# Head gates of an mLSTM layer projected ahead of the heads as 2x2 block products, on one Trainium2 core

## The chip, the core and the metric

One core of a Trainium2 chip runs the whole kernel. The metric is device time in microseconds (us). The kernel before was run three times; its median is the time before. Every profile is one profiled execution. About 0.2% (4.1 us) is what a measurement of this kernel can tell from no change.

## What is computed

Two layers of a hybrid backbone over T = 1152 tokens (128 context, 1024 latent) of width D = 1024. Layer 0 mixes by RG-LRU and Fourier groups, layer 1 by an mLSTM of 8 heads (key width 128, value width 256) that runs in chunks of 128 tokens in both directions. The change is in layer 1:

```python
def mixer_c(h, C0, n0, m0, w_in, b_if, w_out):
    proj = h @ w_in
    q, k, v, o, z, gp = jnp.split(proj, [QK_C, 2*QK_C, 2*QK_C+W_C, 2*QK_C+2*W_C, 2*QK_C+3*W_C], axis=-1)
    ...
    for d in range(2):                     # two directions
        hd, Cd, nd, md = mlstm_chunkwise(fl(q), fl(k), fl(v), fl(gp[:, :, d, 0]), fl(gp[:, :, d, 1]), ...)
        hsum = hsum + fl(hd)
    y = jax.nn.sigmoid(o) * hsum.astype(h.dtype) * jax.nn.silu(z)
    return y @ w_out, ...
```

Per head, o and z are each 256 columns wide: two tiles of 128 columns each. "Pair u" below is o tile u and z tile u, u = 0 to 15, two pairs to a head.

## The kernel before

Activations lie transposed, channels on partitions and the 1152 tokens in the free dimension, for KC = 8 blocks of channels. Every fp32 product is made of three products of fp32r parts: hi by hi, hi by lo, lo by hi. The parts of layer 1's input, `h2hi` and `h2lo` (tiles `h_hi`, `h_lo` in the trace), are made once in the stage `outputs(0, ...)`.

`project` (L116 to L128) makes one output tile of 128 channels by 1152 tokens: 8 blocks times 3 parts times 3 banks of 384 columns, 72 matmuls (L126), into one of two PSUM groups. Its weight tile goes through a ring of two slots: `w_load` (L95, SP) brings 128x1024 into `w_raw`, `w_split_hi` (L102, ACT, the copy in L107) makes `w_hi` when it is loaded and when PE has done with the tile two before (`w_used`), `w_split_lo` (L109, DVE, L111) makes `w_lo`, and `project` waits for `w_lo`. Tiles have sequence numbers: the gate projection (input and forget gates of all heads) is 32, and mLSTM's jobs begin at SEQ0 = 33.

`mlstm()` (L1536 on) runs `body(j, ...)` nine times: body 0 projects head 0 and computes the decays of all heads; body j projects head j and, between its products, does the recurrent work of head j-1; body 8 does the last head's recurrence and its gates. A body's jobs on PE are 0 for q, 1 for k, 2 and 3 for v (`values`, L1867, 256-column matmuls, 72 to a job, both jobs read both v weight tiles) and 4 to 7 for z, o, z, o, by `project`. Nine `step`s (L1832 to L1850: state product and numerators of one chunk in each direction; DVE: L2127 to L2148) stand between the jobs or in a job's middle, so that DVE updates the state while PE projects. ACT (`on_scalar`, L1944 to L2004) takes each product out of PSUM, then splits the tile two further on. The gates: tanh and copy from PSUM by ACT (L1972 to L1975), `gate_z` and `gate_o` on DVE (L2156, L2160) into `out_gate`, which `finish_y` (L2118) multiplies with the turned output. All orders are written out by hand; nothing is scheduled by a program.

Decays: `forget_gates` (L2013 to L2058, with log1p in L551 to L563) is a chain of small operations on `[40, 1152]` rows on DVE, with the splits of v's weight tiles hooked in by name ("inverted", "series_ready", "added"). Its input is the gate projection, copied by ACT to `gate_products` (L2003) and moved to rows by four DMAs (L1674). `gates_to_tokens` (L1786, PE) and `token_scalars` (L2064, DVE) hand the result to the heads.

```python
                    steps(4, 5)
                    split(7)
                    gate(j, 0)
                    steps(6, 7)
                    split(8)
```

These lines of DVE's body before show how weight splits (`split(n)` is `w_split_lo` of job n, n > 7 the next body's) stand between the steps.

Of the kernel before, what the change touches and what calls it, by code (L numbers as in the profile page):

```python
# [14 lines left out]
ds = bass.ds  # L15
# [32 lines left out]
def build(nc, a, out):  # L48
# [253 lines left out]

    def setup():
# [12 lines left out]
        const_in, vec_in, prm_rows_in = sem("const_loaded"), sem("vectors_loaded"), sem("lru_vectors_loaded")  # L316
# [3 lines left out]
        vec_turned, vec_ready = sem("vectors_turned"), sem("vectors_ready")  # L320
        x_turned, xT_dve, xT_act = (sem(s) for s in ("x_turned", "xT_by_dve", "xT_by_act"))
        cond_tanh, cond_ready, zero_ready = sem("cond_tanh"), sem("cond_ready"), sem("zeros_ready")
        x_summed, x_std, x_rstd, x_scaled = (sem(s) for s in (
            "x_rows_squared", "x_rows_std", "x_rows_rstd", "x_rows_scaled"))
        mod_rows, mod_turned, mod_ready, wm_used = (sem(s) for s in (
            "mod_rows_ready", "mod_turned", "mod_ready", "w_mod_used"))
        dve_chain = sem("setup_dve_chain")
# [34 lines left out]
        def on_tensor(pe):  # L362
# [29 lines left out]
            for t in range(NT):  # L392
                pe.wait_ge(x_scaled, t + 1)
# [4 lines left out]
                ins.then_inc(x_turned, 1)  # L398
# [20 lines left out]
        def on_scalar(act):  # L419
# [6 lines left out]
            def x_copy(t):  # L426
                act.wait_ge(x_turned, t + 1)
                act.activation(XT[:, :, t * P:(t + 1) * P].rearrange("p (b k) n -> p b k n", b=2), turned_x(t),
                               ACT.Copy).then_inc(xT_act, 1)
# [24 lines left out]
            for t in range(NT):  # L454
# [5 lines left out]
                act.activation(STD[:, t:t + 1], SSQ[:, t:t + 1], ACT.Sqrt, scale=1.0 / D, bias=EPSB[:]).then_inc(x_std, 1)  # L460
# [23 lines left out]
        def on_vector(dve):  # L484
            ch = Chain(dve, dve_chain)

            def x_copy(t):
                dve.wait_ge(x_turned, t + 1)
# [38 lines left out]
            for t in range(NT):  # L527
                dve.wait_ge(x_std, t + 1)
                dve.reciprocal(STD[:, t:t + 1], STD[:, t:t + 1]).then_inc(x_rstd, 1)
                dve.wait_ge(x_rstd, t + 1)  # L530
                dve.tensor_scalar(XR[:, t, :], XR[:, t, :], STD[:, t:t + 1], None, ALU.mult).then_inc(x_scaled, 1)
# [67 lines left out]
    pads = sem("pads_zero")  # L599
# [600 lines left out]
    def outputs(l, next_tiles):  # L1200
# [32 lines left out]
        def first_products(pe, k0, k1):  # L1233

            if l and k0 == 0:
                pe.wait_ge(mlstm_evacuated, 8 * H)
# [10 lines left out]
        def on_sync(sp):  # L1247
# [54 lines left out]
            if next_tiles:  # L1302
                w_load(sp, *at_seq(SEQ + 2), next_tiles[2])
                w_load(sp, *at_seq(SEQ + 3), next_tiles[3])
# [222 lines left out]

    DK, DV = P, 2 * P
    DV1 = DV + 1
    QCOL, KCOL, VCOL, OCOL, ZCOL = 0, D, 2 * D, 4 * D, 6 * D  # L1530
    SEQ0 = 33
# [9 lines left out]
    def mlstm():  # L1541
# [4 lines left out]
        G = sb("out_gate", [P, 2 * T], at=z)  # L1546
        TO = sb("o_tanh", [P, T], at=z)
        TZ = sb("z_tanh", [P, T], at=z)
        GP_ROWS = sb("gate_products", [P, T], at=list(z))
# [29 lines left out]
        small_in, rows_sb = sem("gate_small_loaded"), sem("gates_in_sbuf")  # L1579
# [26 lines left out]
        def pair(j, n):  # L1606

            if isinstance(j, int):
                return at_seq(SEQ0 + n if j == 0 else SEQ0 + 8 * j - 4 + n - (4 if j == H else 0))
            return j * 4 + (SEQ0 - 4 + n) // 2, (SEQ0 - 4 + n) % 2  # L1610

        def jobs(j):
            return range(4) if isinstance(j, int) and j == 0 else range(4, 8) if isinstance(j, int) and j == H else range(8)

        FIRST_JOBS = {(0, 1): 1, (0, 2): 0, (0, 3): 1, (1, 0): 0, (1, 1): 1}
# [4 lines left out]
        def group_free(eng, j, n):  # L1620
            if isinstance(j, int) and (j, n) == (0, 1):
# [723 lines left out]
```

## Time and profile before

| what | value |
|---|---|
| median of 3 runs | 2047.18 us (2046.47 to 2047.83) |
| span of the profiled execution | 2045.1 us |
| its own time less its span | about 2.1 us, as far as the median tells |
| PE busy | 2010.5 us, 98% of the span |
| DVE, ACT, POOL busy | 1062.9, 652.1 and 106.1 us |

PE is the engine with hardly any idle time. A line of the profile names engine, source line and tiles; "PE MATMUL psum_groups<-h_hi,w_hi" is a product of tokens with weights, the last operand being the stationary one.

### The profile page before, as it was taken

How to read it: one execution, taken by the hardware profiler on the slowest of the kernel's cores; microseconds unless marked ns; L12 is line 12 of the kernel's file. 1: busy time of each engine (PE TensorE's matmuls, PEld its weight loads, DVE VectorE, ACT ScalarE, POOL GpSimd, SP SyncE). 2: the span in 40 equal slices, each digit the busy share in tenths (PEclk: the TensorE clock that was granted, in tenths of full speed). 3: DMA queues.
4: the chain of work that ended last, by engine and by line, in shares of the span. 5: the costliest groups of instructions: out<-in, count | busy, mean ns of one | idle time of the engine just before them, and what ended most of it. 6: DMA issues, size and time to landing. Idle time of an engine off the chain costs nothing.

```text
span 2045.1 us, 28555 instructions
## 1 busy us (share of the span) xinstructions
PE 2010.5 (98%) x11833; PEld 1886.1 (92%) x11833; DVE 1062.9 (52%) x1664; ACT 652.1 (32%) x831; POOL 106.1 (5%) x99
## 2 busy tenths in 40 slices
PE   6999999999999999999999999999999999999998
PEld 5999999999988888999999999999999999998887
DVE  5778788445453575853434335343343433645344
ACT  6677764222234453221111111111121111224422
POOL 0032332000200000000000000000000000000000
PEclk9999999999999999999999999999999999999999
DMA  8221213542246443141222212212122121426554
GB/s 302 68 66 46 74 47 94 184 174 83 73 154 186 154 164 118 42 117 30 83 71 81 62 32 84 70 59 78 38 83 61 48 94 42 104 67 189 170 174 140
DMA packets 218346, 204.62 MB, mean 100 GB/s; under 512 B 13346, under 2 KB 187002, under 8 KB 218098
## 3 DMA queue, kind: packets, MB, share of 16 engines
q1 hardware_dynamic: 214194, 190.52, 30.1%
q0 software_dynamic: 3872, 12.35, 1.8%
q8 instruction: 89, 1.46, 0.3%
q14 instruction: 31, 0.25, 0.0%
q10 hardware_dynamic: 160, 0.05, 0.0%
HBM read 172.14 MB, written 30.59 MB: 99 GB/s over the span
## 4 chain that ended last, share of the span: by engine, by line
PE 93%; ACT 2%; DVE 2%; DMA 1%; issue 1%; SPq 1%; DVEq 0%; ACTq 0%
PE psum_groups L126 48%; PE psum_groups L1229 19%; PE psum_groups L1867 10%; PE psum_groups L1848 3%; PE psum_extra L1839 3%; PE psum_groups L1850 3%; PE psum_groups L1008 1%; PE psum_groups L701 1%; PE psum_groups L144 1%; PE psum_groups L1808 1%; PE psum_groups L998 1%; PE psum_extra L1022 1%; DMA w_mod_rows_a<-in_w_mod 1%; ACT gate_i L762 1%; PE psum_groups L1819 1%
## 5 line engine op out<-in xcount | busy, mean ns | idle before, releaser
L126 PE MATMUL psum_groups<-h_hi,w_hi 128*128 128x384 f32 x1896 | 447.8, 344 | 2.5 <-ACT q_t L1958 1.8
L126 PE MATMUL psum_groups<-h_lo,w_hi 128*128 128x384 f32 x1896 | 434.3, 337 | 0.0
L126 PE MATMUL psum_groups<-h_hi,w_lo 128*128 128x384 f32 x1896 | 434.1, 337 | 0.0
L126 PEld LDWEIGHTS psum_groups<-h_hi,w_hi 128*128 128x128 f32 x1896 | 338.8, 188 | 11.9 <-issue 7.8
L126 PEld LDWEIGHTS psum_groups<-h_lo,w_hi 128*128 128x128 f32 x1896 | 340.5, 188 | 0.0
L126 PEld LDWEIGHTS psum_groups<-h_hi,w_lo 128*128 128x128 f32 x1896 | 340.0, 188 | 0.0
L1229 PE MATMUL psum_groups<-w_out,y_tile_hi 128*128 128x512 f32 x1008 | 317.4, 394 | 0.0
L1229 PEld LDWEIGHTS psum_groups<-w_out,y_tile_hi 128*128 128x128 f32 x1008 | 189.6, 188 | 42.5
L2132 DVE SCALAR_TENSOR_TENSOR state<-state,head_decay,psum_extra 128x257 f32<-128x257 f32 x112 | 54.1, 483 | 287.9 <-PE psum_groups L1850 285.9
L1229 PE MATMUL psum_groups<-w_out,y_tile_lo 128*128 128x512 f32 x504 | 198.1, 393 | 0.0
L1867 PE MATMUL psum_groups<-w_hi,h_hi 128*128 128x256 f32 x576 | 164.4, 285 | 0.0
L1867 PE MATMUL psum_groups<-w_hi,h_lo 128*128 128x256 f32 x576 | 162.5, 282 | 0.0
L1867 PE MATMUL psum_groups<-w_lo,h_hi 128*128 128x256 f32 x576 | 162.3, 282 | 0.0
L111 DVE TENSOR_TENSOR w_lo<-w_raw,w_hi 128x1024 fp32r<-128x1024 f32 x97 | 133.8, 1379 | 47.5 <-ACT w_hi L107 39.1
L107 ACT ACTIVATE w_hi<-w_raw 128x1024 fp32r<-128x1024 f32 x97 | 102.5, 1057 | 46.8 <-PE psum_groups L1867 35.8
L1229 PEld LDWEIGHTS psum_groups<-w_out,y_tile_lo 128*128 128x128 f32 x504 | 94.8, 188 | 20.9
L1867 PEld LDWEIGHTS psum_groups<-w_hi,h_hi 128*128 128x128 f32 x576 | 108.6, 189 | 1.5 <-ACT v_rows L1962 1.5
L1867 PEld LDWEIGHTS psum_groups<-w_lo,h_hi 128*128 128x128 f32 x576 | 108.7, 189 | 0.0
L1867 PEld LDWEIGHTS psum_groups<-w_hi,h_lo 128*128 128x128 f32 x576 | 108.5, 188 | 0.0
L1972 ACT ACTIVATE z_tanh<-psum_groups 128x1152 f32<-128x1152 f32 x16 | 18.1, 1132 | 253.2 <-PE psum_groups L126 253.2
L273 DVE TENSOR_TENSOR y_tile_lo<-y_tile_raw,y_tile_hi 128x512 fp32r<-128x512 f32 x126 | 80.0, 686 | 34.3 <-ACT y_tile_hi L269 33.9
L1848 PE MATMUL psum_groups<-v_rows,decay_matrix 128*128 128x257 f32 x288 | 84.8, 380 | 0.0
(331 smaller groups left out, 2448.0 us busy)
## 6 DMA issues: line engine op xcount, KB each, us to landing
w_raw<-in_w_in_o SPq DMA_DIRECT2D x65, 512.0 KB, 4.9
y_tile_raw<-y_scratch SPq DMA_DIRECT2D x126, 256.0 KB, 3.0
w_raw<-in_w_in_e SPq DMA_DIRECT2D x32, 512.0 KB, 4.0
w_mod_rest<-in_w_mod SPq DMA_DIRECT2D x4, 4096.0 KB, 15.3
y_scratch<-mixed_y POOLq DMA_DIRECT2D x16, 576.0 KB, 3.2
decay_matrix<-gate_rows SPq DMA_DIRECT2D x8, 1152.0 KB, 7.6
q_carry<-gate_rows SPq DMA_DIRECT2D x8, 1152.0 KB, 6.4
y_scratch<-out_gate SPq DMA_DIRECT2D x8, 1152.0 KB, 5.2
```

Of the source, the lines that this page charges most:

```text
L107: act.activation(WHI[:, slot, :], WRAW[:, slot, :], ACT.Copy).then_inc(w_hi, 1)
L111: dve.tensor_tensor(WLO[:, slot, :], WRAW[:, slot, :], WHI[:, slot, :].bitcast(F32), ALU.subtract).then_inc(w_lo, 1)
L126: ins = pe.matmul(PS[:, group, j, 0:JW], w[:, slot, k * P:(k + 1) * P], h(k0 + k)[:, j * JW:(j + 1) * JW], start=start and k == 0 and m == ...
L144: ins = pe.matmul(bank, w[:, slot, k * P:(k + 1) * P], h(k0 + k)[:, g * JW:(g + 1) * JW], start=start and k == 0 and m == 0, stop=stop and ...
L273: eng.tensor_tensor(y_lo_at(l, n, c), y_raw_at(l, n, c), y_hi_at(l, n, c).bitcast(F32), ALU.subtract).then_inc(yo_lo, 1)
L701: ins = pe.matmul(PS[:, what, j, 0:JP + 1], w[:, 2 * what + d, :], x[:, j * JP:(j + 1) * JP + 1], start=m == 0, stop=m == 2)
L1229: ins = pe.matmul(bank(n), y, w[part], start=k == 0 and m == 0, stop=k == 2 * KC - 1 and m == 2)
L1839: ins = pe.matmul(KV[d][:, 0:DV1], KW[:, d, t * P:(t + 1) * P], V[q][:, t, :], start=True, stop=True)
L1848: ins = pe.matmul(NUM[d][:, 0:DV1], DM[q][:, d, cols], V[q][:, t, :], start=True, stop=s == 0)
L1850: ins = pe.matmul(NUM[d][:, 0:DV1], QW[:, d, cols], C[:, d, :], start=False, stop=True)
L1867: ins = pe.matmul(dst, h[:, k, t * P:(t + 1) * P], w[:, slot, cols], start=k == 0 and m == 0 and n % 2 == 0, stop=k == KC - 1 and m == 2, ...
L2132: ins = dve.scalar_tensor_tensor(C[:, d, :], C[:, d, :], DC[:, d, tiles[d]:tiles[d] + 1], KV[d][:, 0:DV1], ALU.mult, ALU.add)
```

## The change

It adds a stage `o_z_gates()` between layer 0's outputs and `mlstm()`. There the gates of heads 0 to 6 (pairs 0 to 13) are computed and stored in DRAM (`gate_scratch`); mLSTM loads two pairs per head. Pair 0 is made by two plain products. Pairs 1 to 13 are each a 2x2 block product, (o and z columns) by (two halves of the channels) by (two halves of the tokens), by the Strassen-Winograd scheme: 7 products of 512 channels by 128 columns by 576 tokens (24 matmuls of 288 columns each) where two plain ones took 8 quarter products of that size. Four sums of token quarters are made once (128x2304 each, hi and lo), four sums of weights for every pair, and five sums of the products. Head 7's gates stay where they were. Bodies 0 to 7 have 4 jobs instead of 8 (q, k, v, v), and the nine steps are set inside these jobs. The gate projection goes through DRAM on its way to rows. DVE and SP begin mLSTM after the stage's last product.

```diff
-    def project(pe, pair, slot, group, hi, lo, k0=0, start=True, stop=True, ready=None, middle=None, ks=range(KC)):
+    def project(pe, pair, slot, group, hi, lo, k0=0, start=True, stop=True, ready=None, middle=None, ks=range(KC), at=None):
...
+            if at and k in at:
+                at[k]()
...
+        MOVING = [(tokens(H2HI, 0, FIRST_Q), tokens(H2LO, 0, FIRST_Q)), (THI[T2], TLO[T2]), (THI[T1], TLO[T1]),
+                  (tokens(H2HI, 1, FIRST_Q), tokens(H2LO, 1, FIRST_Q)), (THI[T3], TLO[T3]),
+                  (tokens(H2HI, 1, SECOND_Q), tokens(H2LO, 1, SECOND_Q)), (THI[T4], TLO[T4])]
...
+        def on_gpsimd(pool):
+            outputs_over(pool)
+            pool.tensor_tensor(TRAW[T1][:], tokens(H2LO, 0, SECOND_Q).bitcast(F32), tokens(H2LO, 0, FIRST_Q).bitcast(F32),
+                               ALU.subtract).then_inc(t_pool[0], 1)
+            pool.wait_ge(*since(t_lo, 1))
+            pool.tensor_tensor(TRAW[T4][:], tokens(H2HI, 1, FIRST_Q).bitcast(F32), TRAW[T4][:], ALU.subtract
+                               ).then_inc(t_pool[0], 1)
...
+            project(pe, *at_seq(34), 1, h2hi, h2lo)
+            for u in range(1, GU):
+                for p in range(PRODUCTS):
...
+                    for k in range(4):
+                        for m, (wn, hn) in enumerate(((0, 0), (0, 1), (1, 0))):
+                            for j in range(2):
+                                ins = pe.matmul(BANKS[p][:, j, :], w[wn][:, k * P:(k + 1) * P],
+                                                h[hn][:, k, j * JQ:(j + 1) * JQ], start=OPENS[p] and k == 0 and m == 0,
+                                                stop=k == 3 and m == 2, skip_group_check=True)
+                    ins.then_inc(product_done[0], 1)
...
+        def on_vector(dve):
...
+            for u in range(1, GU):
+                if u > 1:
+                    combined(u - 1, 5)
+                operand(u, 4)
+                if u > 1:
+                    z_part(u - 1)
+                operand(u, 5)
+                combined(u, 1)
...
-    SEQ0 = 33
+    SEQ0 = 35
...
         def on_sync(sp):
-            outputs_over(sp)
+            gates_over(sp)
...
+                elif qkv:
+                    job(0, {4: turn_k})
+                    scores()
+                    job(1, {3: turn_before, 5: do_step(0)})
+                    do_step(1)()
+                    job(2, {2: do_step(2), 4: do_step(3), 6: do_step(4)})
+                    do_step(5)()
+                    job(3, {3: do_step(6), 6: do_step(7)})
+                    do_step(8)()
...
-                    at_hooks = {"inverted": 3, "series_ready": 4, "added": 5}
+                    at_hooks = {"inverted": 2, "series_ready": 3, "scanned": 4}
...
-            outputs_over(dve)
+            gates_over(dve)
...
+            dve.wait_ge(gate_stored, 16 * GU)
             run(dve, body, Heads())
```

Where the instructions go, at three places.

DVE at the start of the new stage, behind layer 0's last pieces. `token_sum_218`, `220`, `221` are raw sums of token quarters (T1, T3 and T4, T4's buffer holding T2 first), `token_sum_lo_215` is the lo part of T2, `weight_sum_222` and `223` sums of quarters of the o and z weights, which lie in `w_raw` here; L1791 makes a lo part of a weight operand.

```order
L1487 TENSOR_TENSOR h_lo<-psum_extra,h_hi 128x8x128 [waits h2_hi_ready]
L111 TENSOR_TENSOR w_lo<-w_raw,w_hi 128x1024 [waits w_hi_ready]
L1825 TENSOR_TENSOR token_sum_220<-h_hi 128x2304 [waits h2_lo_ready,x_stored]
L1825 TENSOR_TENSOR token_sum_220<-token_sum_220,h_lo 128x2304 [waits setup_then_gate_dve_chain] x2
L1825 TENSOR_TENSOR token_sum_221<-token_sum_220,h_hi 128x2304 [waits mod_turned_then_token_sum_ready]
L1825 TENSOR_TENSOR token_sum_221<-token_sum_221,h_lo 128x2304 [waits setup_then_gate_dve_chain]
L1780 TENSOR_TENSOR weight_sum_222<-w_raw 128x512 [waits vectors_loaded_then_o_z_weights_loaded_1]
...
L1791 TENSOR_TENSOR strassen_weights_lo<-w_raw,strassen_weights_hi 128x512 [waits x_rows_rstd_then_strassen_weights_hi,x_rows_scaled_then_weight_sum_ready]
...
L1795 TENSOR_TENSOR token_sum_lo_215<-token_sum_221,token_sum_hi_211 128x2304 [waits cond_tanh_then_token_sum_hi]
L1791 TENSOR_TENSOR w_lo<-weight_sum_223,w_hi 128x512 [waits x_rows_rstd_then_strassen_weights_hi]
L1825 TENSOR_TENSOR token_sum_218<-token_sum_218,h_hi 128x2304 [waits vectors_ready_then_token_sum_by_pool]
...
L1791 TENSOR_TENSOR w_lo<-weight_sum_222,w_hi 128x512 [waits x_rows_rstd_then_strassen_weights_hi]
```

None of these rows exists before, where memsets of mLSTM's rows follow layer 0's last row (there L1478) and the `L111`. Each lo of a token sum stands behind ACT's hi of the same sum, and the two raw operations on T1 (`token_sum_218`, one shown) behind the first lo.

DVE in a head's last steps, before. A pair of `state` rows opens a step, a pair of `h_rows` rows ends it; the split is that of job 7, and the gates of a pair follow it.

```order
L2132 SCALAR_TENSOR_TENSOR state<-state,head_decay,psum_extra 128x257 [waits mlstm_dve_chain]
...
L2145 SCALAR_TENSOR_TENSOR h_rows<-psum_groups,inverse_den,h_rows 128x256 [waits mlstm_dve_chain]
...
L2145 SCALAR_TENSOR_TENSOR h_rows<-psum_groups,inverse_den,h_rows 128x256 [waits mlstm_dve_chain]
...
L111 TENSOR_TENSOR w_lo<-w_raw,w_hi 128x1024 [waits w_hi_ready]
...
L2156 SCALAR_TENSOR_TENSOR out_gate<-z_tanh,out_gate 128x1152 [waits projection_evacuated]
...
L2160 SCALAR_TENSOR_TENSOR out_gate<-o_tanh,out_gate 128x1152 [waits mlstm_dve_chain]
...
L2132 SCALAR_TENSOR_TENSOR state<-state,head_decay,psum_extra 128x257 [waits numerator_done]
...
L2132 SCALAR_TENSOR_TENSOR state<-state,head_decay,psum_extra 128x257 [waits mlstm_dve_chain]
```

The same engine at the same steps in the changed kernel: steps 5 and 6 of a head of the loop.

```order
L2503 SCALAR_TENSOR_TENSOR state<-state,head_decay,psum_extra 128x257 [waits numerator_done]
...
L2516 SCALAR_TENSOR_TENSOR h_rows<-psum_groups,inverse_den,h_rows 128x256 [waits mlstm_dve_chain]
...
L2516 SCALAR_TENSOR_TENSOR h_rows<-psum_groups,inverse_den,h_rows 128x256 [waits mlstm_dve_chain]
...
L111 TENSOR_TENSOR w_lo<-w_raw,w_hi 128x1024 [waits w_hi_ready]
...
L2503 SCALAR_TENSOR_TENSOR state<-state,head_decay,psum_extra 128x257 [waits numerator_done]
...
L2503 SCALAR_TENSOR_TENSOR state<-state,head_decay,psum_extra 128x257 [waits mlstm_dve_chain]
...
L2516 SCALAR_TENSOR_TENSOR h_rows<-psum_groups,inverse_den,h_rows 128x256 [waits mlstm_dve_chain]
...
L2516 SCALAR_TENSOR_TENSOR h_rows<-psum_groups,inverse_den,h_rows 128x256 [waits mlstm_dve_chain]
```

The split between steps 5 and 6 is now that of the next body's first tile, and the gates are gone.

## Rows read from the trace of the kernel before

**Rows 1.** The page: the span, then busy time of PE.

```profile
span 2045.1 us, 28555 instructions
...
PE 2010.5 (98%) x11833; PEld 1886.1 (92%) x11833; DVE 1062.9 (52%) x1664; ACT 652.1 (32%) x831; POOL 106.1 (5%) x99
```

**Rows 2.** The page's chain of waits: shares of the span by engine and line.

```profile
PE psum_groups L126 48%; PE psum_groups L1229 19%; PE psum_groups L1867 10%; PE psum_groups L1848 3%; PE psum_extra L1839 3%; PE psum_groups L1850 3%; PE psum_groups L1008 1%; PE psum_groups L701 1%; PE psum_groups L144 1%; PE psum_groups L1808 1%; PE psum_groups L998 1%; PE psum_extra L1022 1%; DMA w_mod_rows_a<-in_w_mod 1%; ACT gate_i L762 1%; PE psum_groups L1819 1%
```

**Rows 3.** The chain of waits in order of time (start, us, what).

```profile
711.65 10.90 PE psum_groups L1229 x48
...
813.31 12.67 PE psum_groups L126 x72
...
882.09 2.61 PE psum_groups L1808 x18
...
1009.92 2.01 PE psum_groups L1808 x18
...
1141.17 8.54 PE psum_groups L1867 x72
...
1656.49 2.01 PE psum_groups L1808 x18
```

**Rows 4.** DVE's groups by form (count, busy us, mean ns, idle before, releasers).

```profile
L111 DVE TENSOR_TENSOR w_lo<-w_raw,w_hi 128x1024 fp32r<-128x1024 f32 x97 | 133.8, 1379 | 47.5 <-ACT w_hi L107 39.1 <-issue 4.1 <-DVE q_carry L2109 1.5
L273 DVE TENSOR_TENSOR y_tile_lo<-y_tile_raw,y_tile_hi 128x512 fp32r<-128x512 f32 x126 | 80.0, 686 | 34.3 <-ACT y_tile_hi L269 33.9
...
L2160 DVE SCALAR_TENSOR_TENSOR out_gate<-o_tanh,out_gate 128x1152 f32<-128x1152 f32 x16 | 21.7, 1358 | 0.5
...
L2109 DVE TENSOR_TENSOR q_carry<-q_carry,q_t 128x2304 f32<-128x2304 f32 x8 | 20.4, 2553 | 1.0 <-DMA q_carry<-gate_rows 1.0
```

**Rows 5.** ACT's groups by form.

```profile
L107 ACT ACTIVATE w_hi<-w_raw 128x1024 fp32r<-128x1024 f32 x97 | 102.5, 1057 | 46.8 <-PE psum_groups L1867 35.8 <-PE psum_groups L144 9.2 <-DMA w_raw<-in_w_in_e 1.8
L269 ACT ACTIVATE y_tile_hi<-y_tile_raw 128x512 fp32r<-128x512 f32 x126 | 72.1, 623 | 21.6 <-DMA y_tile_raw<-y_scratch 20.7
...
L1944 ACT ACTIVATE decay_matrix<-decay_matrix 128x2304 f32<-128x2304 f32 x8 | 17.1, 2133 | 73.3 <-DVEq L2078 73.3
```

**Rows 6.** Timeline of DVE and POOL in layer 0 (start, us, engine, line).

```profile
138.13 4.38 POOL L640 TENSOR_TENSOR tanh_then_state<-tanh_then_state 128x128 f32<-128x128 f32 x2 [22.04 <-DVE lru_final L883]
...
140.16 3.42 DVE L111 TENSOR_TENSOR w_lo<-w_raw,w_hi 128x1024 fp32r<-128x1024 f32 x1
...
142.67 3.20 POOL L645 TENSOR_TENSOR mixed_y<-tanh_then_state,z_silu 128x128 f32<-128x128 f32 x2 [0.16 <-POOL tanh_then_state L640]
```

**Rows 7.** POOL's groups by form.

```profile
L645 POOL TENSOR_TENSOR mixed_y<-tanh_then_state,z_silu 128x1024 f32<-128x1024 f32 x8 | 16.4, 2056 | 0.0
```

**Rows 8.** Timeline of DVE, the decays' chain.

```profile
811.46 0.07 DVE L2264 MEMSET v_rows<- 128x9 f32 x1
...
820.25 0.81 DVE L2016 TENSOR_SCALAR rows_f<-rows_f,row_b_f 40x1152 f32<-40x1152 f32 x1 [3.30 <-DMA row_m<-in_state_mlstm_m]
...
833.04 1.23 DVE L111 TENSOR_TENSOR w_lo<-w_raw,w_hi 128x1024 fp32r<-128x1024 f32 x1
...
848.81 1.22 DVE L111 TENSOR_TENSOR w_lo<-w_raw,w_hi 128x1024 fp32r<-128x1024 f32 x1
```

**Rows 9.** Timeline of ACT, in the same stretch.

```profile
822.28 1.28 ACT L1984 ACT_TABLE_LOAD   x1
```

**Rows 10.** Windows: start:end, length, busy PE, PEld, DVE, ACT, POOL, granted clock, DMA share, GB/s.

```profile
875.00:880.00 5.00, 3.92 (x40) 3.55 (x39) 0.98 (x7) 3.02 (x4) 3.06 (x7) 0.98 0.59 89
880.00:885.00 5.00, 5.00 (x31) 5.00 (x32) 4.83 (x10) 0.00 (x0) 0.56 (x1) 0.68 0.49 180
```

**Rows 11.** Timeline of DVE, one step of a head.

```profile
1312.29 1.00 DVE L2132 SCALAR_TENSOR_TENSOR state<-state,head_decay,psum_extra 128x257 f32<-128x257 f32 x2 [5.29 <-PE psum_groups L1850]
...
1313.79 1.00 DVE L2148 TENSOR_SCALAR h_rows<-psum_groups,inverse_den 128x256 f32<-128x256 f32 x2
```

More of the change, by code:

```diff
@@ L1851, in step, with values @@
                 ins.then_inc(num_done, 1)
-            def values(j, first, last, done, middle=None):
+            def values(j, first, last, done, at):
                 for k in range(KC):
@@ L1876, in body, with job @@
                 h, q = j - 1, 1 - p
-                def job(n, middle=None):
-                    if n not in jobs(j) or isinstance(j, int) and j == 0 and n == 0:
+                def job(n, at={}):
+                    if n not in jobs(j):
                         return
@@ L1883, in job @@
                     if n == 2:
-                        values(j, 0, 6, va_done, middle)
+                        values(j, 0, 6, va_done, at)
                     elif n == 3:
-                        values(j, 6, 9, None)
+                        values(j, 6, 9, None, at)
                     else:
-                        project(pe, *pair(j, n), group_of(j, n), h2hi, h2lo, middle=middle)
-                def steps(*some):
-                    if ml:
-                        for s in some:
-                            step(h, q, s, post)
@@ new lines, in body @@
+                    forget_gates(lambda at: at in at_hooks and split(at_hooks[at]))
+                elif not post:
+                    split(1)
+                    token_scalars()
+                    split(2)
+                    exponents(h, q)
+                    weigh_k(h, False)
+                    dve.memset(V[1][:, :, DV:DV1].rearrange("p t o -> p (t o)"), 1.0).then_inc(ones_ready, 1)
+                    split(3)
+                    dve.wait_ge(dec_in, 16)
+                    decay_of(h)
+                    weigh_scores(h, q)
+                    steps(0, 1, 2, 3)
+                    exponents(j, p, (0,))
+                    steps(4)
+                    split(4)
+                    exponents(j, p, (1,))
+                    steps(5, 6, 7, 8)
+                elif qkv:
+                    split(1)
+                    weigh_k(h)
@@ L2210, in body @@
-                    split(8)
-                    exponents(j, p)
-                    steps(8)
-                    if not (isinstance(j, int) and j == H - 1):
-                        gate(j, 1)
+                    split(2)
+                    steps(1)
+                    split(3)
+                    steps(2)
+                    exponents(j, p, (0,))
+                    steps(3)
+                    exponents(j, p, (1,))
+                    steps(4, 5)
+                    split(4)
+                    steps(6, 7, 8)
@@ L2244, in body @@
                         y_split_lo(dve, 1, t, 2)
[L2246 removed]
+            LINKS = 58
             class Heads:
```

569 lines of the change are left out of this document (412 added, 157 removed).

## The prediction

> **What bounds the kernel now.** I read the page first: PE is busy for 2010.5 of 2045.1 us [rows 1], so only work taken off PE, or waits put on it, can move the time. The page's chain of waits says which work: 48% of the span is `project` (L126), and 32 of its projections, 406 us at 12.68, are gates of the heads; few lines of another engine are in it [rows 2]. The chain in order of time then gives prices on PE: a plain projection takes 12.67 us for 72 matmuls of 384 columns, 176 ns each; 72 matmuls of 256 columns take 8.54 us, 118.6 ns each; 48 of 512 columns 10.90 us, 227.1 ns each [rows 3]. Last the groups and timelines of DVE, ACT and POOL, since the new stage and the rearranged heads live by what these three deliver in time [rows 4 to 9]. The sum is made against the profiled execution's span, 2045.1 us; the median is 2.1 above it and I add that at the end.
>
> **The products.** A pair was two projections, 2 x 12.68 = 25.36 us. It becomes 7 x 24 = 168 matmuls of 288 columns. No row has 288 columns; between 256 and 384 the price rises by 57.5 ns in 128 columns, so 288 lies at 118.6 + 14.4 = 133.0 ns (on the line from 256 to 512 at 132.2; a chain of small pieces might cost 136). I take 133.0: 22.35 us a pair, 3.0 us less, and for 13 pairs **-39.0 us**. With 132.2 it is -41, with 136 -33. Pair 0 costs what it did.
>
> **The stall that goes.** PE stood still for some 3.2 us before the first head's scores at 882.09, while DVE turned token scalars, and for the next 5 us its granted clock was 0.68, between its two levels of 1.2 and 2.4 GHz; the scores took 2.61 us where later heads show 2.01 [rows 3, 10]. The change puts the transposes between two projections, which covers this: **-4.5 us**, bounds 0 and -5.
>
> **The start of the new stage.** PE has two plain projections in hand and would reach the first block product at 813.31 + 12.67 = 826.0. DVE is free at 811.5 [rows 8]. Before the first weight operand it has five sums of 128x2304 at 2.55 us (the only row of that size, L2109), three 128x512 at 0.69, and waits for links: done at about 826.5 [rows 4], so 0.5 us is lost. Product 1 needs T2: its raw form is ready at 824.3, but ACT first makes a weight hi that waits for the sum at 827.1, then T2's hi in 2.13 us (L1944), then DVE its lo in 2.55 and a weight lo in 0.69: 833.2 against 829.7, 3.5 us [rows 4, 5]. Product 2 needs T1: two more sums, hi and lo, 5.1 + 0.2 + 2.1 + 2.6 = 10.0 us more, against 3.2 us of PE work: 6.8. T3's lo fits. Products 5 and 6 wait for sums of products that stand behind T4's lo and the gate operations of pair 0 (2 x 1.36): 2.6 and 1.6. Together **+15.1 us**.
>
> POOL's part of the sums comes on top. A POOL operation of 128x1024 takes 2.06 us alone [rows 7], so 2304 columns take 4.64. In layer 0 a w_lo subtraction on DVE, 1.23 us normally, took 3.42, and ended about when POOL's pair of operations ended (142.5) [rows 6]: a DVE operation with two inputs in SBUF stood still while POOL ran. The Trainium skill states this as a rule (SBUF — State Buffer, Who interferes with whom): "A DVE instruction with two SBUF inputs contends with a GpSimd instruction that reads SBUF", one holding the lock for its whole length. By it and the row alike, POOL's first sum runs while DVE idles before 810.3, and the other two, which wait for T2's lo, fall where DVE is what PE waits for: **+9.3 us**; 0 if they interleave without loss, 12 at most with the 3.42 us row's stretch.
>
> **Steady pairs.** For each pair DVE has 11 operations of 512 columns (0.69), five sums out of PSUM of 576 columns (about 0.78 by the same slope) and two gate operations (1.36): 14.1 of 22.35 us. ACT has 7 hi copies at 0.62 and 2 tanh and a copy, 7 us. I cost them at nothing; their cover is the products before, three or four products ahead (10 us). If one turn of the chain product, sum, next product into the same bank (0.8 us plus signals) were not covered, it would cost 1 us a pair.
>
> **From the stage to the heads.** In the kernel before the decays' chain ran from 811.5 beside PE's projections of head 0, and only 28.6 us passed from its first operation (820.25) to the second hook (848.81) [rows 8]. Now DVE waits for the last product, the last gates (0.8 + 1.1 + 2.7 us), and their way to DRAM (some 5 us) before it starts: the first row operation comes about 15.5 us after the last product. The hooks moved up by one, since head 0's first tile is now split earlier; so the lo of the first v tile comes at 15.5 + 12.8 - 1.3 + 1.2 (an ACT table load of 1.28 goes [rows 9]) = 28.2 against PE's 25.4 + 0.8, a stall of 2.1; the next v tile's lo at 15.5 + 27.3 + 1.2 = 44.0 against 28.3 + 4.3 + 4.3 = 36.8, 7.2. With 0.8 for the first lo: **+10.2 us**, bounds 3 and 16.
>
> **Head 0's recurrence** (body 1). The next body's first weight split now stands before step 5's state on DVE. Its hi waits until PE has used v's first tile, which happens after k = 3 of job 3, while PE's step 6 stands at k = 4: from there hi 1.06, lo 1.23, two additions for exponents 2.7, step 5 in 2.5 us [rows 4, 5, 11]: 7.0, and 1.1 for smaller waits: **+8.1 us**, bounds 3 and 10.
>
> **Six later heads.** The same split stands between steps 5 and 6. After k = 3 of job 3 PE has two blocks of k, 2 x 1.07 = 2.14 us, before step 7, while ACT and DVE need 1.06 + 1.23 + 2.0 for hi, lo and enough of step 6: 2.15 us lost there, 0.63 at step 8: 2.8 us a head, **+16.7 us**, bounds 0 and 20. The other steps are covered by 3 to 4 us of blocks each. The unstalled body keeps its price: 129.3 us a head between the scores of one and of a later one ((1656.49 - 1009.92) / 5) less 4 x 12.68 is 78.6 [rows 3]; the gates' store and load (1.2 MB a head each way) lie beside 45 us of products and 80 us of a head.
>
> **Rest.** After two idles as long as that before 882 (T1's, and the v tile's) the clock will fall as it did there, 1.6 us each: +3.2. The last body waits for a y store more: +0.8.
>
> **Sum.** -39.0 - 4.5 + 15.1 + 9.3 + 10.2 + 8.1 + 16.7 + 3.2 + 0.8 = +19.9: span 2065.0, median 2067.
>
> **Rivals.**
> A, forecast: waits given back exceed what the products save. 2061 to 2073. Chance 0.40.
> B, POOL and DVE do not exclude each other here, or the stage's start is shorter: 2067 - 9.3 = 2058. For it: only three POOL operations. Against: [rows 6]. With those parts of the heads' stalls that come out low, 2051 to 2061. Chance 0.22.
> C, a steady stall: one turn through a bank uncovered, +1.0 us x 13 = 2080, up to 2085. For it: three sums a pair each gate the next product. Chance 0.14.
> D, other side: the split in a head's last steps costs nothing. Its place is DVE between steps 5 and 6, its price 16.7 + 8.1; it decides once v's first tile is released 3 us earlier or DVE has 3 us of slack on PE's step 7. With the start's stalls halved as well (-12): 2067 - 24.8 - 12 = 2030; the first alone 2042. For it: before, DVE was idle 5.3 us before a step [rows 11]. Against: the release stands in the code behind k = 3. Chance 0.08.
> E, other side by the product's pace: if 288 columns take 120 ns, as pure streaming at 2.4 GHz, 2184 x 13 ns = 28.5 us go: 2039; below 124 ns it decides. Against: 384 columns take 176 ns, not 160 [rows 3]. Chance 0.06. The Trainium skill (TensorE: Matmul & The Clock Gate, Back-to-back issue gap) gives N / 2.4 + 2.5 ns for a warm product alone, which would be an estimated 122.5 ns for 288 columns and a sum of 2044; it gives 162.5 for 384, and the trace shows 176.
> F: the terms meet in the middle, 2043 to 2051. Chance 0.10.
>
> **Numbers.** Likeliest is A: 2067. The range holds A, B, F's upper part and most of C: 2045 to 2081. Leaving out D and E (0.14) and edges of C and F. Faster by over 0.2% (below 2043.1): D, E, less what of them lies above, 0.12. Within 0.2%, which is about what a measurement of this kernel can tell from no change (2043.1 to 2051.3): 0.09. Slower: 0.79.
>
> **What would show it.** In the changed profile: the 24 matmuls of a product in 3.19 us; PE idle before products 1, 2, 5 and 6 of pair 1, some 25 us until pair 2, with POOL's operations 4.6 us long beside a stretched DVE one; windows of later pairs with PE full; PE idle 2 and 7 us before v's two tiles in body 0; 7 us before step 6 of body 1, and 2.8 us in every loop head. The prediction is wrong if the 288-column matmul takes under 128 or over 138 ns, if heads come at 78.6 us instead of 81.4, or if the stage's start costs under 12 us.

## The result, and the profile after

The changed kernel takes 2072.79 us (median of 4 runs, 2072.31 to 2075.02) against 2047.42 us for the kernel before on the same chip: a ratio of 1.0126, 95% interval 1.0112 to 1.0141, 25 us slower. Forecast were 2067 us, slower, and a range of 2045 to 2081.

The page of the changed kernel, first its totals and then the head of its chain of waits by engine and line:

```profile
span 2071.6 us, 29611 instructions
...
PE 1983.4 (96%) x12145; PEld 1855.5 (90%) x12145; DVE 1208.0 (58%) x1857; ACT 686.5 (33%) x913; POOL 124.1 (6%) x102
...
PE 85%; DVE 9%; ACT 3%; issue 2%; DMA 1%; ACTq 0%; DVEq 0%; SPq 0%
```

PE is busy 27 us less than before [rows 1] and the span is 26.5 us longer, so PE now stands idle for over 50 us more. PE's share of the chain that ended last is 85%; DVE has 9% of it. "issue" is time in which an engine waited for nothing that the profile shows.

The waits of PE from the start of the new stage to the end of head 0's recurrence (waiting line, releaser, us in total, times, longest):

```profile
PE psum_groups L1692 <- issue: 14.6, 1, 14.6
PE psum_groups L2235 <- DVE w_lo L111: 7.7, 2, 6.9
PE psum_extra L2207 <- DVE state L2503: 6.4, 1, 6.4
PE psum_extra L1692 <- DVE w_lo L1791: 3.1, 1, 3.1
PE psum_extra L1692 <- DVE z_projection L1806: 1.2, 1, 1.2
```

And from there to the last head:

```profile
PE psum_extra L2207 <- DVE state L2503: 7.5, 6, 1.3
PE psum_groups L128 <- issue: 6.6, 2, 4.8
PE psum_groups L2216 <- DVE h_rows L2516: 5.6, 12, 0.6
```

The first row of the upper view is the wait before product 2 of pair 1, 14.6 us; the view puts it down to "issue", but the timelines show what came last, the two sums of T1. DVE's, and below it POOL's, with its first operation of that size, beside which DVE had nothing to do:

```profile
831.37 2.56 DVE L1795 TENSOR_TENSOR token_sum_lo<-token_sum,token_sum_hi 128x2304 fp32r<-128x2304 f32 x1 [2.78 <-ACT token_sum_hi L1712]
833.85 0.69 DVE L1791 TENSOR_TENSOR w_lo<-weight_sum,w_hi 128x512 fp32r<-128x512 f32 x1
834.45 14.79 DVE L1825 TENSOR_TENSOR token_sum<-token_sum,h_hi 128x2304 f32<-128x2304 f32 x2
849.17 0.68 DVE L1791 TENSOR_TENSOR w_lo<-weight_sum,w_hi 128x512 fp32r<-128x512 f32 x1
...
851.43 2.56 DVE L1795 TENSOR_TENSOR token_sum_lo<-token_sum,token_sum_hi 128x2304 fp32r<-128x2304 f32 x1 [0.99 <-ACT token_sum_hi L1712]
```

```profile
803.05 5.17 POOL L1659 TENSOR_TENSOR token_sum<-h_lo 128x2304 f32<-128x2304 f32 x1 [218.36 <-DVE h_lo L1487]
...
834.01 5.51 POOL L1662 TENSOR_TENSOR token_sum<-h_hi,token_sum 128x2304 f32<-128x2304 f32 x1 [25.80 <-DVE token_sum_lo L1795]
839.60 7.23 POOL L1665 TENSOR_TENSOR token_sum<-token_sum,h_lo 128x2304 f32<-128x2304 f32 x1
```

Two operations that take 5.15 us elsewhere on this engine took 14.79, and ended 2.4 us after POOL's second operation, one DVE operation's time. The products themselves are as forecast, in the chain in order of time 3.18 us for 24 matmuls, 132.6 ns each [rows 3 have the neighbours]:

```profile
886.28 3.18 PE psum_extra L1692 x24
889.46 3.17 PE psum_groups L1692 x24
892.63 3.19 PE psum_extra L1692 x24
...
1183.53 19.94 PE psum_groups L2235 x144
...
1456.43 4.80 issue
```

The last two rows here are head 0's values from v's second tile on (I had written 72 matmuls to a job; job 2 has 144, whose second half stands here, and job 3 has 72), which took 19.94 us for 144 matmuls where 118.6 ns each would be 17.1, and a wait of 4.8 us in the heads that no engine released, where the kernel before had one of 0.6. It stands where heads 2 and 3 have been done and the engines jump back to the start of the loop. Windows around it (start:end, length, busy PE, PEld, DVE, ACT, POOL, granted clock, DMA share, GB/s):

```profile
1454.00:1457.00 3.00, 2.00 (x8) 1.81 (x9) 0.28 (x1) 0.00 (x0) 0.00 (x0) 0.76 0.68 232
1457.00:1460.00 3.00, 0.00 (x0) 0.00 (x0) 0.00 (x0) 0.00 (x0) 0.00 (x0) 0.50 0.92 320
...
1463.00:1466.00 3.00, 3.00 (x11) 3.00 (x11) 0.00 (x0) 0.00 (x0) 0.00 (x0) 0.53 1.03 393
1466.00:1469.00 3.00, 3.00 (x22) 2.96 (x21) 0.15 (x1) 0.00 (x0) 0.00 (x0) 1.00 0.74 242
```

DVE waits there in one piece:

```profile
1460.85 1.22 DVE L111 TENSOR_TENSOR w_lo<-w_raw,w_hi 128x1024 fp32r<-128x1024 f32 x1 [6.57 <-issue]
```

PE and DVE both have nothing to do while the DMA engines fill up, and the clock is at its lower level of 1.2 GHz (0.50) for the rest of that idle time and the first microseconds of work behind it, as in [rows 10].

Against the steps of the forecast, from the profile's own rows:

| step | forecast us | measured us |
|---|---|---|
| 13 pairs as 7 products | -39.0 | -40.1 (91 x 3.182 for 13 x 25.36) |
| the stall before the first head's scores | -4.5 | -2.9 (a wait of 1.1, then transposes in 2.19 for 0.99 and scores in 2.61 for 2.01) |
| start of the stage, POOL and low clock in it | +15.1 + 9.3 + 1.6 | +23.7 (827.58 to 1140.86, less 289.6) |
| first tiles of head 0: waits | +10.2 | +8.4 (0.7, 0.8, 6.9) |
| low clock behind the last of these | +1.6 | +2.9 (19.94 - 17.1) |
| head 0's recurrence | +8.1 | +7.4 |
| six later heads | +16.7 | +13.1 (7.5 + 5.6) |
| code after the jump | none | +9.2 (89.9 us for that head, 80.7 for its neighbours) |
| layer 0 and its setup, which the change leaves alone | 0 | +1.6 |

The rows add up to +23.3, the span to +26.5. Of the 3.2 us between them 2.5 are low clock in head 0's recurrence, behind the wait of 6.4 us: 12 matmuls in 5.09 us that take 2.59 in later steps.

### The profile page after: what moved, and what is told of

It reads as the page before. It is cut to its first block, busy times and chain, and to the rows that moved or that the text cites. A ratio compares the mean times of both kernels' runs of the same rounds, so it can differ in the third digit from the quotient of the medians.

```text
span 2071.6 us, 29611 instructions
## 1 busy us (share of the span) xinstructions
PE 1983.4 (96%) x12145; PEld 1855.5 (90%) x12145; DVE 1208.0 (58%) x1857; ACT 686.5 (33%) x913; POOL 124.1 (6%) x102
## 4 chain that ended last, share of the span: by engine, by line
PE 85%; DVE 9%; ACT 3%; issue 2%; DMA 1%; ACTq 0%; DVEq 0%; SPq 0%
PE psum_groups L128 29%; PE psum_groups L1239 19%; PE psum_groups L2235 8%; PE psum_groups L1692 7%; PE psum_extra L1692 6%; PE psum_groups L2216 3%; PE psum_groups L2218 3%; PE psum_extra L2207 2%; PE psum_groups L1018 2%; PE psum_groups L711 1%; DVE token_sum L1825 1%; PE psum_groups L146 1%; PE psum_groups L1008 1%; ACT w_hi L107 1%; PE psum_extra L1032 1%
## 5 line engine op out<-in xcount | busy, mean ns | idle before, releaser
L128 PE MATMUL psum_groups<-h_hi,w_hi 128*128 128x384 f32 x1272 | 298.0, 342 | 5.1 <-DVE h_lo L529 2.2
L128 PE MATMUL psum_groups<-h_hi,w_lo 128*128 128x384 f32 x1272 | 291.4, 336 | 4.8 <-issue 4.8
L128 PE MATMUL psum_groups<-h_lo,w_hi 128*128 128x384 f32 x1272 | 291.0, 336 | 0.0
L128 PEld LDWEIGHTS psum_groups<-h_hi,w_hi 128*128 128x128 f32 x1272 | 225.4, 189 | 14.5 <-issue 11.4
L128 PEld LDWEIGHTS psum_groups<-h_lo,w_hi 128*128 128x128 f32 x1272 | 228.4, 188 | 0.0
L128 PEld LDWEIGHTS psum_groups<-h_hi,w_lo 128*128 128x128 f32 x1272 | 228.0, 188 | 0.0
L2235 PE MATMUL psum_groups<-w_hi,h_hi 128*128 128x256 f32 x576 | 173.0, 300 | 7.7 <-DVE w_lo L111 7.7
L111 DVE TENSOR_TENSOR w_lo<-w_raw,w_hi 128x1024 fp32r<-128x1024 f32 x71 | 102.1, 1438 | 65.4 <-ACT w_hi L107 56.4
L107 ACT ACTIVATE w_hi<-w_raw 128x1024 fp32r<-128x1024 f32 x71 | 75.0, 1056 | 70.3 <-PE psum_groups L2235 60.1
L292 DVE TENSOR_TENSOR w_out<-w_out_raw,w_out 128x1024 fp32r<-128x1024 f32 x28 | 34.2, 1224 | 86.1 <-ACT w_out L287 86.1
```

The lines of the kernel that those rows point to most:

```text
L107: act.activation(WHI[:, slot, :], WRAW[:, slot, :], ACT.Copy).then_inc(w_hi, 1)
L111: dve.tensor_tensor(WLO[:, slot, :], WRAW[:, slot, :], WHI[:, slot, :].bitcast(F32), ALU.subtract).then_inc(w_lo, 1)
L128: ins = pe.matmul(PS[:, group, j, 0:JW], w[:, slot, k * P:(k + 1) * P], h(k0 + k)[:, j * JW:(j + 1) * JW], start=start and k == 0 and m == ...
L2235: ins = pe.matmul(dst, h[:, k, t * P:(t + 1) * P], w[:, slot, cols], start=k == 0 and m == 0 and n % 2 == 0, stop=k == KC - 1 and m == 2, ...
```

## The experiments

Each is the changed kernel with one edit, timed against the kernel before. The start of layer 1 varies by some 1.7 us between profiled executions with nothing changed ahead of it, so I read waits from the rows and take the span for a check only. The times of e1, e3, e4, e5 and e7 lie within 4.1 us of the changed kernel's, the least that a measurement can tell; what these five show is in their rows.

**e1, the gate load late.** The stall at the jump: is it the gate load, the one new transfer there?

```diff
                 if qkv and ml:
-                    load_gate(h, 1 - p)
                     load_weights_of(j, p)
...
+                if qkv and ml:
+                    load_gate(h, 1 - p)
```

> Only SP's order changes: the 1.2 MB load of a head's gates is issued after the body's weight loads instead of ahead of the next head's decay matrix. Theory (after the jump back to the loop's start PE and DVE wait for code, whose DMA packets share saturated DMA engines with the gate load): the stall of PE between 1452 and 1461 us of the changed kernel (1.8 and 4.8 us) shrinks to under 2 us in all, close to the 0.6 us of the kernel before, and with the low clock behind it the span falls by 5 to 9 us, to some 2063 to 2066. Rival (the stall comes of the jump itself, of the shorter body, or of where in the body it stands, whatever else the DMA engines carry): the stall stays at 6 us or more and the span within 2 us of 2071.6.

2074.23 us; ratio 1.0136 (1.0119 to 1.0153). The span is 2071.4 and the stall is there:

```profile
PE psum_groups L128 <- issue: 6.5, 2, 4.3
```

```profile
1454.00:1457.00 3.00, 2.27 (x8) 2.08 (x9) 0.00 (x0) 0.00 (x0) 0.00 (x0) 0.73 0.70 246
1457.00:1460.00 3.00, 0.00 (x0) 0.00 (x0) 0.00 (x0) 0.00 (x0) 0.00 (x0) 0.50 1.00 358
```

The theory in this form is wrong: 6.5 us remain. But the run could not part the two theories as well as I had meant, since the next loads moved up and kept the DMA engines just as full (DMA share 0.70 and 1.00).

**e2, the splits behind a step.**

```diff
                     steps(4)
-                    split(4)
                     exponents(j, p, (1,))
-                    steps(5, 6, 7, 8)
+                    steps(5)
+                    split(4)
+                    steps(6, 7, 8)
...
-                    steps(4, 5)
+                    steps(4, 5, 6)
                     split(4)
-                    steps(6, 7, 8)
+                    steps(7, 8)
```

> In the six later heads DVE's split of the next head's first weight tile stands behind step 6 instead of ahead of it; in the first head's recurrence it stands behind step 5, with the second half of the exponents ahead of step 5. Theory (DVE waits in order for a weight tile that PE releases behind block k = 3, and the steps queue behind it): the stalls of 1.25 + 0.37 + 0.62 us per later head and of 6.4 us in the first vanish or fall under 0.5 us a head and 1 us in the first; a later head comes at 78.4 instead of 80.7 us; the span falls by 13.4 + 6 + 1.5 of low clock = 18 to 21 us, to some 2051 to 2054. Rival (the steps are paced by DVE's own 2.5 us and PE's waits only move to another step or to the next head's first job): the sum of PE's idle time per head stays at 2 us, span within 4 us of 2071.6.

2052.64 us; ratio 1.0024 (1.0014 to 1.0033); span 2051.2. The waits of PE from 1250 to 1800 us:

```profile
PE psum_groups L128 <- issue: 6.9, 2, 4.9
PE psum_groups L2216 <- DVE h_rows L2516: 4.2, 8, 0.6
PE psum_groups L128 <- ACT o_tanh L2354: 2.0, 1, 2.0
```

The row behind `o_tanh` stands in the last body; e3 has it too (2.1 us, against 0.4 in the changed kernel), and its cause stays open. The rows "L2207 <- DVE state" (6.4 and 7.5 us) are gone, and what waits for h_rows is 4.2 us of all heads, of which 0.4 to 0.6 a head at step 8. Two misplaced calls had cost 20 of the 25.4 us by which the change is slower; the theory holds, its numbers too.

**e3, one hook earlier.** v's second tile of head 0.

```diff
             ch.link(dve.scalar_tensor_tensor(E, E, 1.0 / (2 * m + 1), S2, ALU.add, ALU.mult))
+            if between and m == 7:
+                between("first_term")
...
-                    at_hooks = {"inverted": 2, "series_ready": 3, "scanned": 4}
+                    at_hooks = {"inverted": 2, "first_term": 3, "scanned": 4}
```

> The lo of head 0's second v weight tile stands one operation into the series of the decays' chain instead of behind the series. Theory: it is ready at about 1174 us of the profile instead of 1183.5, before PE needs it at 1176.6, so the stall of 6.9 us and the low clock behind it go; nothing else in the chain waits for PE: span down by 7 to 9 us, to 2063 to 2065. Rival (the chain, not the tile, is what the heads wait for: the first head's exponents and transposes then come late by as much): the stall reappears before the first head's transposes or scores, span within 2 us of 2071.6.

2075.06 us; ratio 1.0133 (1.0116 to 1.0150); span 2074.8. PE's timeline shows the wait one tile on:

```profile
1200.67 1.30 PE L128 MATMUL psum_groups<-h_hi,w_hi 128*128 128x384 f32 x3 [7.01 <-DVE w_lo L111]
```

The 6.9 us before v's second tile are gone and 7.0 us stand before the next head's first tile, whose lo is the next in DVE's order, behind the scans. My theory was wrong, the rival right in its outcome: nothing was won. It had the place wrong, though, which is not the chain's end. The span is 3.2 us longer, outside the rival's 2 us; the last body begins at 1786.1 us in both profiles, and the 3.2 us come behind that, 1.7 of them in the wait for `o_tanh`.

**e4, POOL's part of T4 on DVE.**

```diff
-            pool.wait_ge(*since(t_lo, 1))
-            pool.tensor_tensor(TRAW[T4][:], tokens(H2HI, 1, FIRST_Q).bitcast(F32), TRAW[T4][:], ALU.subtract
...
             token_lo(3, T3)
+            ch.link(dve.tensor_tensor(TRAW[T4][:], h(H2HI, 1, FIRST_Q), TRAW[T4][:], ALU.subtract))
+            tt(TRAW[T4], TRAW[T4][:], h(H2LO, 1, FIRST_Q), ALU.add).then_inc(t_pool[0], 2)
```

> The two POOL operations that finish the token sum T4 are made by DVE instead, behind T3's lo. Theory (a POOL operation that reads SBUF and a DVE operation with two SBUF inputs exclude each other): DVE's two operations on T1 take 5.1 us instead of 14.8, DVE has 5.1 us more of its own, product 2 starts after a stall of 6 to 7 us instead of 14.6, later products of the first pair wait up to 5 us more, and the stage's start costs 4 to 6 us less; span 2065 to 2068. Rival (they share without loss and the 14.8 us have another cause, such as the size or the operands): the two operations stay near 14.8 us and the span rises by about 5 us, to 2077.

2071.14 us; ratio 1.0119 (1.0102 to 1.0136); span 2068.6. DVE at the same two sums of T1, and the two that it has now:

```profile
833.92 5.14 DVE L1819 TENSOR_TENSOR token_sum<-token_sum,h_hi 128x2304 f32<-128x2304 f32 x2
838.98 0.68 DVE L1785 TENSOR_TENSOR w_lo<-weight_sum,w_hi 128x512 fp32r<-128x512 f32 x1
...
846.80 2.55 DVE L1846 TENSOR_TENSOR token_sum<-h_hi,token_sum 128x2304 f32<-128x2304 f32 x1
849.45 2.56 DVE L1819 TENSOR_TENSOR token_sum<-token_sum,h_lo 128x2304 f32<-128x2304 f32 x1
```

5.14 us instead of 14.79, with POOL silent: the two engines excluded each other. POOL's two operations had cost DVE 9.65 us, as the forecast had it (9.3); DVE's own work for them is 5.1. The wait before product 2 is 4.9 us, but products 4 and 5 now wait 2.0 and 1.9 us. The last product of the stage ends 4.0 us earlier from its start (1136.29 - 827.05 against 1140.86 - 827.58), as forecast (4 to 6), though its waits fell by 7.1 us: the granted clock is 0.71 and 0.66 in the windows from 855 to 865, behind the new waits, and about 3 us go back that way.

**e5, SP's burst 6 us later.**

```diff
                     sp.wait_ge(num_done, h * 9)
+                    sp.wait_ge(ks_done, h * 6 + 1)
```

> SP's burst of loads between two heads (decays of q, state, gates, decay matrix, weights: 4.4 MB) waits for the first transposes of the next head, 6 us behind the jump back to the loop's start, instead of for the last numerators, which come at the jump. Theory A (code that PE and DVE need behind the jump is fetched by DMA and stands behind this burst; taking the gate load alone out left the other loads to fill the engines): the stall of 1.8 + 4.8 us falls to under 2.5 us in all, the low clock behind it goes, span down by 5 to 8 us, to 2064 to 2066. Theory B (the stall belongs to the jump, whatever the DMA engines do): it stays at 6 us or more. Either way the loads are still in time, since the decays of q are used 17 us after their issue and take 6.4.

2069.64 us; ratio 1.0111 (1.0096 to 1.0127); span 2067.6. Waits, then windows:

```profile
PE psum_groups L128 <- issue: 3.0, 2, 2.3
```

```profile
1452.00:1455.00 3.00, 2.08 (x8) 2.09 (x9) 0.39 (x2) 0.00 (x0) 0.00 (x0) 0.74 0.04 8
1455.00:1458.00 3.00, 2.23 (x8) 2.04 (x7) 1.41 (x3) 0.00 (x0) 0.00 (x0) 0.50 0.03 8
```

3.0 us in place of 6.6, at a DMA share of 0.04. By queue, the stretch from 1449 to 1456 of this run holds instruction packets and nothing else:

```profile
q8 instruction: 2, 0.03, 2.6%
q14 instruction: 2, 0.02, 0.7%
```

while in the changed kernel from 1452.5 to 1458 the one queue with packets is that of the data:

```profile
q1 hardware_dynamic: 215, 0.99, 56.9%
```

There the instruction packets come between 1458.5 and 1459.5, and DVE and PE go on at 1460.85 and 1461.23:

```profile
q8 instruction: 1, 0.02, 6.0%
q14 instruction: 1, 0.01, 1.9%
```

Theory A holds in kind: code behind the jump comes by DMA, and behind a burst it comes late. It is worth 3.6 us of wait; 3.0 us stay that no burst explains (I had asked for under 2.5). The low clock stayed too (0.50, then 0.62 up to 1461), so the head behind the jump takes 86.6 us, for 89.9 and the 80.6 of its neighbours, and the span fell by 4.0 us where I expected 5 to 8.

**e6, heads 2 to 5 written out.**

```diff
-            with eng.Fori(1, H // 2 - 1) as m:
+            for m in range(1, H // 2 - 1):
```

> Heads 2 to 5 are written out instead of run in a loop of two turns: the same instructions, no jump back. Theories A and B both say that the stall of 1.8 + 4.8 us at 1452 to 1461 goes, since code then comes in order ahead of time; the head that follows comes 80.7 us after the one before instead of 90, span down by 8 to 10 us, to 2062 to 2064. A third theory, C (code of the straight-line heads too is fetched late when the burst comes): idle time of PE put down to issue stays in one head or appears in others.

2064.78 us; ratio 1.0084 (1.0069 to 1.0100); span 2064.0. The same view as for the changed kernel:

```profile
PE psum_extra L2207 <- DVE state L2503: 7.5, 6, 1.3
PE psum_groups L2216 <- DVE h_rows L2516: 5.2, 12, 0.6
```

The row "issue" is gone and no other took its place; theory C falls. The burst is still there, and PE works through it (from 1456 to 1459 it is busy all the time, at a granted clock of 1.00 and a DMA share of 0.98). The head at that place takes 80.6 us for 89.9. Two later heads take 81.9 instead of 80.6: their waits of 1.25 and 0.37 us are those of the changed kernel, but here the granted clock fell behind them (0.80 from 1524 to 1528, 0.78 for the next 4 us). One head of e5, whose loop is not written out, does the same. The span is 2064.0, the upper end of the forecast.

The jump is what asks for code late, the burst what makes it later.

**e7, two hooks and the transposes inside the k projection.**

```diff
-                    at_hooks = {"inverted": 2, "series_ready": 3, "scanned": 4}
+                    at_hooks = {"inverted": 2, "first_term": 3, "added": 4}
...
-                    gates_to_tokens()
-                    job(1, {4: turn_k})
+                    job(1, {3: gates_to_tokens, 6: turn_k})
```

> After the run that moved only one hook, the wait stood at the next head's first tile (7.0 us). Here that tile's lo stands ahead of the maximum scans too, and the first head's transposes of scalars stand inside its k projection. Theory (the decays' chain itself ends late, and PE can work two more projections before it needs it): the 6.9 us before v's second tile go, the next wait is for the chain's exponentials inside the k projection, 0 to 3 us, and another 0 to 3 us for scores with less cover: span down by 3 to 8 us, to 2064 to 2068. Rival (the chain is the bound to its end; PE only meets it later): the sum of idle time between 1140 and 1265 us stays at 8 us or more, span within 2 us of 2071.6.

2069.28 us; ratio 1.0113 (1.0098 to 1.0129); span 2067.1.

```profile
1209.81 1.33 PE L128 MATMUL psum_groups<-h_hi,w_hi 128*128 128x384 f32 x3 [4.05 <-ACT q_t L2341]
```

Both tile waits are gone. A new one of 4.05 us stands before head 1's k projection, at a place that I had not named: ACT takes q out of PSUM only after the four exponentials, for which it waits for the chain's end. 3 us are won.

**e8, the edits of e2, e4, e5 and e7 together**, with all token sums made by DVE and begun early:

```diff
-            w_split_lo(dve, *at_seq(34))
             outputs_over(dve)
             ch.link(tt(TRAW[T3], h(H2HI, 1, SECOND_Q), h(H2HI, 0, SECOND_Q), ALU.subtract))
...
+            w_split_lo(dve, *at_seq(34))
...
+            ch.link(tt(TRAW[T1], h(H2LO, 0, SECOND_Q), h(H2LO, 0, FIRST_Q), ALU.subtract))
```

> The moved splits of the second run, DVE's sums of the fourth, the hooks and transposes of the one before, SP's later burst, and besides: DVE makes all of the token sums and begins them when layer 0's outputs are stored, at 803 us, ahead of the split of z's tile. If the parts add up: from the 2051.2 us of the second run less 4 (sums), less 5 to 9 (nine idle microseconds of DVE used, 2.6 us of POOL's first sum added), less 3 to 8 (hooks), less 5 to 8 (burst): span 2024 to 2035, which is under the kernel before by 10 to 21 us, with the products' gain of 39 us in it. If waits only move from one place to the next, it stays above 2040.

2035.60 us; ratio 0.9946 (0.9932 to 0.9959); span 2034.9, at the upper end of what I had expected. It is faster than the kernel before, with the 4.06 us before k's projection still in it, and 6.7, 2.4, 2.0 and 1.2 us at the stage's start.

**e9, q out of PSUM before the exponentials.**

```diff
                 if ml:
                     w_split_hi(act, *pair(j, jobs(j)[0] + 1))
-                if ml and not post:
-                    act.wait_ge(args_ready, 1)
...
+                    if n == 0 and ml and not post:
+                        act.wait_ge(args_ready, 1)
```

> The version with all parts together, and ACT takes head 1's q out of PSUM before it waits for the decays' arguments, instead of after. In the version before, PE waited 4.1 us for that copy at the start of the k projection. Theory: that wait goes, the transposes inside the k projection may wait up to 1.5 us for the exponentials, and the low clock behind it goes: span 2034.9 less 3 to 5, 2030 to 2032. Rival (the decays' chain itself is what PE waits for there, wherever it stands): the 4 us reappear at the transposes, span within 1 us of 2034.9.

2032.92 us; ratio 0.9928 (0.9915 to 0.9942); span 2032.8: 2 to 3 us less than e8, a little under the forecast of 3 to 5, and less than the 4.1 us that times alone can tell. The row shows what happened:

```profile
1203.71 0.77 PE L128 MATMUL psum_groups<-h_hi,w_hi 128*128 128x384 f32 x3 [1.93 <-DVE w_lo L111]
```

The wait of 4.06 us for the copy is gone and no wait stands at the transposes, so the rival falls; in its place PE waits 1.9 us for the lo of head 1's k tile, which stands behind the chain's last operations on DVE.

**e10, and the heads written out**: the edits of e9 and of e6.

```diff
-            with eng.Fori(1, H // 2 - 1) as m:
+            for m in range(1, H // 2 - 1):
```

> The same, with heads 2 to 5 written out. Theory: what is left of the wait for code at the jump (1.9 + 0.8 us, and the low clock behind it) goes: 3 to 5 us under the looped version, span 2025 to 2029, a ratio of about 0.990 to 0.992 to the kernel before. Rival (longer code is fetched late somewhere else): as slow as the looped version or slower.

2027.52 us; ratio 0.9901 (0.9886 to 0.9916); span 2026.9, in the forecast range, and 5.4 us less than e9. The largest waits left on PE from the new stage on (the first is that before product 2; "issue" at the jump is gone):

```profile
PE psum_groups L1686 <- issue: 6.9, 1, 6.9
PE psum_groups L2214 <- DVE h_rows L2513: 4.5, 8, 0.6
PE psum_groups L128 <- DVE w_lo L111: 2.6, 2, 1.9
PE psum_extra L1686 <- DVE strassen_u L1796: 2.2, 1, 2.2
```

This version beats both kernels: 19.9 us under the one before, 45 under the change as made. The block products are worth their 40 us, of which about half is now in the time.

## Why the prediction was right

Sign and cause were right: the time lies 5.8 us above the forecast and in the range, because waits given back exceed what the products save (case A). That the total came so near is in part luck: five terms (products, start, first tiles, both places of the splits) came out better than forecast by 9.5 us together, and the jump, which has no term, cost 9.2. What is left above the forecast is low clock (2.5 us in head 0's recurrence, 1.3 more than forecast at v's second tile), a stall of before that was worth 1.6 less, and the 1.6 us of layer 0.

- **Products.** 133.0 ns forecast, 132.6 measured; -40.1 us for -39.0. Case E, products at a streaming pace of 120 ns, falls. The estimate of 122.5 ns from the Trainium skill (TensorE: Matmul & The Clock Gate, Back-to-back issue gap), whose formula is for a product alone, lies 10 ns under the measured 132.6. Interpolating between two rows of the same kernel was the better guide.
- **Start of the stage.** 26.0 with its low clock against 23.7 measured. Product 1 waited 3.1 us (3.5), product 2 14.6 (6.8 + 9.3), products 5 and 6 1.2 in all where I had 4.2: the longer wait at product 2 had given the sums behind it time. POOL's exclusion of DVE is shown by e4, 9.65 us for 9.3; case B falls. The trace agrees with the Trainium skill's rule (SBUF — State Buffer, Who interferes with whom) that a DVE instruction with two SBUF inputs contends with a GpSimd instruction that reads SBUF: 14.79 us beside POOL's, 5.14 without. The size of the term was off in its parts: a POOL operation of 2304 columns takes 5.17 us with DVE idle, not the 4.64 scaled from [rows 7], and DVE was still at a weight lo when the first of the two began.
- **The stall that went.** PE did not stand still for 3.2 us before 882.09: it waited for 1.08 us and then made nine transposes, in 2.19 us for 0.99, as the granted clock fell. The term of -4.5 was worth -2.9, and the premise of the low-clock term ("two idles as long as that") falls with it, since there the clock fell behind a wait of 1.08 us.
- **Steady pairs.** The waits of the first pair are all that the view shows in the stage, and no pause in the other twelve is over 0.2 us; case C falls.
- **From the stage to the heads.** 8.4 for 10.2, and the place as named. That moving the hook would not have helped is what e3 showed and the prediction did not ask.
- **The splits in the heads.** 7.4 for 8.1 and 13.1 for 16.7, both removed by e2. Case D, the other side, named this as the price that decides: had the splits stood well, the kernel would still have been 0.2% slower (e2). It took e4, e5 and e7 besides to get under the time before (e8); whether e2 and e6 alone would do it, as their savings of 20 and 8 us suggest, no run shows. So D with splits alone, 2042, was too low by 10 us.
- **What failed.** The step "The unstalled body keeps its price", with the gates' loads "beside 45 us of products and 80 us of a head", held for five heads of six. The jump back to the loop's start cost 9.2 us in the sixth, waits of 6.6 and the low clock behind. The rows for it were in the trace of before, PE's and DVE's at the same jump, and I passed over them as small:

```profile
1242.02 0.79 PE L126 MATMUL psum_groups<-h_hi,w_hi 128*128 128x384 f32 x3 [0.63 <-issue]
...
1249.82 1.23 DVE L111 TENSOR_TENSOR w_lo<-w_raw,w_hi 128x1024 fp32r<-128x1024 f32 x1 [4.13 <-issue]
```

DVE stood still there too: the loads began at the jump too (DMA share 0.69 to 1.03 from 1242 to 1251), one instruction packet came at 1242 and the next ones only at 1247 to 1249. Why PE had work to go on with for all that time, and has not in the changed kernel, stays open; no run tried it.
- **Low clock.** 3.2 us forecast for two idles; product 1 (4.87 us for 3.18), products 2 and 3 (2.1), v's second tile (2.9) and the head after the jump (2.6) together show some 9, and head 0's recurrence 2.5 more.

## What to carry to other kernels

When work leaves a loop that it used to pad, ask of every in-order instruction that stays what now stands right before it: here a split of a weight tile that waited for PE cost 20 us once the projections around it were gone, and moving one line at each of two places gave it back. Moving a wait's cause earlier wins only as far as the next item in the same queue allows (e3 won nothing, e7 3 us), so follow the queue to its end before editing. Don't give POOL a share of elementwise work while DVE's two-input operations set the pace: 9.65 us of DVE's time went for 5.1 us of work, though giving it back won only 4.0 us of the stage (e4).

## What the hardware showed that I had not expected

Behind a jump back in a long hardware loop PE and DVE each stood 6.6 us with nothing that released them. From 1452.5 to 1458 no packet of the instruction queues moved while 0.99 MB of data did; the packets came up to 1459.5, and both engines went on at about 1461. With the data held back PE's wait was 3.0 us, without a jump there was none. POOL's own operations of 128x2304 took 5.5 and 7.2 us beside DVE's, against 5.17 with DVE idle: the exclusion cost both sides. The granted clock fell behind waits as short as 1.08 us (before, at 879.90) and 1.25 and 0.37 us (e6), and in other heads the same waits left it at full.
